# Expert blocks in order of their counts, narrow blocks with high and low halves side by side, their down projection in plain fp32

## The chip, the cores and the metric

One core of one Trainium2 chip runs the whole program. The metric is the device time of one execution in microseconds; three executions of the kernel before took 2009.57, 2016.96 and 2018.43 us (median 2016.96).

## The reference, cut to what matters

Two mixer layers (state space, window and forgetting attention), a third hybrid layer, and behind it a mixture of 32 experts over 256 tokens. The change is in the mixture alone, apart from the few steps just ahead of it:

```python
# t: 256 x 1024; w_gate, w_up: 32 x 1024 x 512; w_down: 32 x 512 x 1024
combine = two chosen experts of each token (softmax weights), zero for the other 30
for e in range(32):
    hid = silu(t @ w_gate[e]) * (t @ w_up[e])
    out = out + combine[:, e:e + 1] * (hid @ w_down[e])
```

So 512 (token, expert) pairs exist. Each expert's three matrices are 2 MB each and are read from HBM once for each block of rows that uses them.

## The kernel before

**Routing.** The 512 pairs are sorted by expert: VectorE counts the pairs of each expert (a matmul sums the one-hot rows), a scan gives each expert's offset, and `slots_of` makes two 256-column halves of a 0/1 matrix that says which token stands at which sorted place. TensorE (`select`, L1078) multiplies the tokens by it into `xs`: all 512 sorted rows, transposed, in a high and a low half of fp32r. The low half is what fp32r's rounding left over, so a product is three fp32r matmuls (hi by hi, hi by lo, lo by hi; L668 to L670).

**Blocks.** There are 35 blocks of 128 sorted rows: block x below 32 is the start of expert x, and three more (`route_more`) take the rows of experts with over 128. `move_window` copies the 128 columns of block x out of `xs` into one of two windows: the high half on ScalarE, the low half on VectorE.

**Units.** A block's step on TensorE has 12 units of weights, each [128 x 1024] floats (512 KB): 4 of `w_gate[x]` (i = 0 to 3), 4 of `w_up[x]` (i = 4 to 7), and 4 of `w_down` of the block before (i = 8 to 11). A unit is 6 matmuls of 512 columns: 2 k x 3 for gate and up (window stationary, weights moving), 2 output halves x 3 for down. At i = 2 the hidden rows of block x - 1 are transposed (`turn_hidden`, 4 transposes); at i = 3 ScalarE copies them as high half (`hid_hi`) and VectorE makes the low half (`hid_lo`); the down units at i = 8 wait for that.

**Halving.** ScalarE casts each unit's high half (`high_half`, L2415 with L2425), VectorE subtracts for the low half (`low_half`, L1835 with L1173). Both run through the steps in the program's order, 6 units (`LOOK`) ahead of TensorE; the ring of halves has 8 places. In a step ScalarE and VectorE do these in a fixed order: for VectorE the low half that is due, then (i = 8) the product of gate and up, then (i = 3) the hidden rows' low half.

**Loads.** SyncE issues every load, in order, 1 MB (two units) each, into 6 slots: for each x gate of x, up of x, down of x - 1 (`load_half`, L2750). A load waits until VectorE has halved both units that lay in its slot, which are the same matrix's of one block before. The first three loads are issued during the stage before (`bridge`, with the first 4 units halved there too), four more as buffers come free, before the routing is known.

**Output.** ScalarE and VectorE copy the two down banks; POOL scatters the rows to HBM (`store_rows`), and at the end gathers them; VectorE adds them with their weights.

Of the kernel before, what the change touches and what calls it, by code (L numbers as in the profile page):

```python
# [2 lines left out]

# [5 lines left out]
F32 = mybir.dt.float32  # L9
F32R = mybir.dt.float32r  # L10
BF16 = mybir.dt.bfloat16
I32 = mybir.dt.int32
# [40 lines left out]
MORE = 3  # L53
BLOCKS = EXP + MORE
SLOTS = 2 * S
SLOT_QUARTERS = SLOTS // 256
LAST_START = SLOTS - P
UNITS_OF = 12
N_UNITS = UNITS_OF * BLOCKS
RING, LOOK, EARLY = 8, 6, 4  # L60
# [143 lines left out]
def build(nc, d, out):  # L204
    ctx = ExitStack()
    with ctx:  # L206
# [57 lines left out]
        more_ready, hid_hi_made = (sem(n) for n in ("more_ready", "hid_hi_made"))  # L264
# [262 lines left out]
        def unit_halves(u):  # L527
            tiles = w_halves + [(y_hi, y_lo), (y_hi, y_lo), (h_hi, h_lo), (h_hi, h_lo)]
            hi, lo = tiles[u % RING]
            c = D if u % RING in (5, 7) else 0  # L530
            return hi[:, c:c + D], lo[:, c:c + D]

# [15 lines left out]
        def stationary(x):  # L548
            return tuple(a[:, :, 0:P] for a in xs) if x == 0 else windows[x % 2]
        hid = [R[1][:, i * FF:(i + 1) * FF] for i in range(2)]  # L550
# [5 lines left out]
        hid_t = [(over_tile(f"hid_hi{i}", FF, "r1", D + i * FF), over_tile(f"hid_lo{i}", FF, "r0", i * FF)) for i in range(2)]  # L556
        y_out = [merged[:, i * D:(i + 1) * D] for i in range(2)]
# [3 lines left out]
        more_hot = bias_rows[0][:, 0:96].rearrange("p (j e) -> p j e", j=MORE)  # L561
        of_expert = bias_rows[0][:, 96:204].rearrange("p (q e) -> p q e", q=3)
        offset, count = (of_expert[:, i, 0:EXP] for i in range(2))
        offset_all, count_all = (of_expert[:, i, 0:BLOCKS] for i in range(2))
# [3 lines left out]
        reach, over, rank = bias_rows[0][:, 432:464], bias_rows[0][:, 464:496], bias_rows[1][:, 80:112]  # L568
# [3 lines left out]
        more_wide = scratch[2][:, 0:3 * MORE * EXP].rearrange("p (q j e) -> p q j e", q=3, j=MORE)  # L572
        more_sums = bias_rows[1][:, 360:369].rearrange("p (q j) -> p q j", q=3)
        more_i = bias_rows[1][:, 372:372 + MORE].bitcast(I32)
# [4 lines left out]
        counting = consts[:, CH:2 * CH]  # L579
# [34 lines left out]
        def tensor_program(e):  # L614
# [448 lines left out]
            def moe():  # L1063
# [12 lines left out]
                e.matmul(bank[:, 2 * EXP:3 * EXP], ones, m1, start=False, stop=True).then_inc(full[b], 1)  # L1076
# [11 lines left out]
                def turn_hidden(x):  # L1088
                    await_drained(("up", x))
                    b, bank = take(turned, ("hid", x))  # L1090
                    for k in range(4):
                        done = e.transpose(bank[:, k * P:(k + 1) * P], hid[x % 2][:, k * P:(k + 1) * P], ident)
                    done.then_inc(full[b], 1)
# [3 lines left out]
                e.wait_ge(ht_lo_made, 2 * T)  # L1097
                early = Banks([0, 1, 2, 3, 4, 5, 6])
                for f in range(8):
                    select(0, f, early)  # L1100
                for x in range(BLOCKS + 1):
                    for i in range(units_in(x)):
# [14 lines left out]
                        e.wait_ge(m_lo, u + 1)  # L1117
                        hi, lo = unit_halves(u)
                        if x < BLOCKS and i < 8:
                            for j in range(2):  # L1120
                                k = 2 * (i % 4) + j
                                done = product(bank_up[:, :], tuple(a[:, k, :] for a in stationary(x)),
                                               (hi[:, j * FF:(j + 1) * FF], lo[:, j * FF:(j + 1) * FF]), k == 0, k == KD - 1)
                        else:
                            k = i % 4
                            for n, (b, bank) in enumerate(got):
                                done = product(bank[:, :], tuple(a[:, k * P:(k + 1) * P] for a in hid_t[(x - 1) % 2]),
                                               (hi[:, n * CH:(n + 1) * CH], lo[:, n * CH:(n + 1) * CH]), k == 0, k == 3)
# [29 lines left out]
        def vector_program(v):  # L1158
# [676 lines left out]
            def low_half(u):  # L1835
                v.wait_ge(m_hi, u + 1)
                hi, lo = unit_halves(u)
                tt(lo, unit_raw(u), hi.bitcast(F32), SUB, m_lo)
# [7 lines left out]
            def bridge():  # L1846
# [4 lines left out]
                for u in range(EARLY):  # L1851
                    low_half(u)
# [8 lines left out]
            def route():  # L1861
# [35 lines left out]
                o.did(v.tensor_copy(of_expert[:, 2, 0:EXP], index_row), mask_ready)  # L1897
                for q in range(len(QUARTERS)):
                    low_quarter(q)
                b, n, bank = await_full(("count",))  # L1900
                total = bank[:, T * EXP:(T + 1) * EXP]
                o.did(v.tensor_tensor_scan(reach, unit_row[:, 0:1].to_broadcast([P, EXP]), total, 0.0, MUL, ADD))
                o.did(v.tensor_copy(count, total))
                o.prev()
                tt(offset, reach, count, SUB)
                o.prev()
                tt(tok(place), tok(bank[:, 0:T * EXP]), offset.unsqueeze(1).to_broadcast([P, T, EXP]), ADD, drained[b], n)
                o.prev()
# [17 lines left out]
            def route_more():  # L1926

                ts(over, count, 128.0, None, ALU.is_gt)
                o.prev()
                o.did(v.tensor_tensor_scan(rank, unit_row[:, 0:1].to_broadcast([P, EXP]), over, 0.0, MUL, ADD))  # L1930
                o.prev()
                tt(rank, rank, over, MUL)
                o.prev()
                tt(more_hot, rank.unsqueeze(1).to_broadcast([P, MORE, EXP]), bc(unit_row[:, 0:MORE], EXP), ALU.is_equal)
                o.prev()
                tt(more_wide, of_expert[:, :, 0:EXP].unsqueeze(2).to_broadcast([P, 3, MORE, EXP]), more_hot.unsqueeze(1).to_broadcast([P, 3, MORE, EXP]), MUL)
                o.prev()
                o.did(v.tensor_reduce(more_sums, more_wide, AX, ADD))
                o.prev()
                ts(offset_all[:, EXP:BLOCKS], more_sums[:, 0, :], 128.0, None, ADD)  # L1940
                ts(count_all[:, EXP:BLOCKS], more_sums[:, 1, :], -128.0, None, ADD)
                o.did(v.tensor_copy(more_i, more_sums[:, 2, :]), more_ready)
                o.prev()

            def starts():

                ts(start_f, offset_all, float(LAST_START), None, MIN)
# [42 lines left out]
            def move_window(x):  # L1990
# [4 lines left out]
                start = v.value_load(start_i[0:1, x:x + 1], min_val=0, max_val=LAST_START)  # L1995
                if x >= 2:
                    v.wait_ge(m_used, first_unit(x - 2) + 8)
                v.tensor_copy(windows[x % 2][1], xs[1][:, :, bass.DynSlice(start, P)]).then_inc(window_lo, 1)

            def moe():  # L2000
# [3 lines left out]
                for f in range(1, 8, 2):  # L2004
                    fill(0, f)
                for u in range(EARLY, LOOK):
                    low_half(u)
                slots_of(1)
                route_more()
                starts()  # L2010
                weighing = weights()
                next(weighing)
                late = []
                for x in range(BLOCKS + 1):
                    for i in range(units_in(x)):
                        u = first_unit(x) + i
                        if u + LOOK < N_UNITS:
                            low_half(u + LOOK)
# [84 lines left out]
        def scalar_program(a):  # L2103
# [311 lines left out]
            def high_half(u):  # L2415
# [5 lines left out]
                elif u < 6:  # L2421
                    await_full((("out2", 1), 1))
                else:
                    await_full(("router",))
# [466 lines left out]
```

## Time and profile before

| | |
|---|---|
| median of 3 runs | 2016.96 us |
| profiled execution: its own time / its span | 2012.43 us / 2010.3 us |
| mixture: first product of block 0 / first of block 1 / end of the last | 1384.0 / 1403.7 / 1990.1 us from the span's start |
| TensorE busy, whole span | 94% |
| mean granted TensorE clock | 0.983 |
| read from HBM | 406.5 MB |

Slices 28 to 39 of the page's 40 (50 us each) are the mixture. "Busy" of TensorE is by modelled ends: a matmul's record overlaps the next, so the distance from start to start is its cost. The trace times count from the span's start.

### The profile page before, as it was taken

The numbers are of one execution on the slowest core, as the hardware profiler recorded it, in microseconds if no ns is written. First come the engines' busy times: TensorE is split into PE (matmuls) and PEld (weight loads), VectorE is DVE, ScalarE is ACT, GpSimd is POOL, SyncE is SP. The second block draws the span as 40 slices with busy tenths as digits, with TensorE's granted clock in tenths as the row PEclk, the third lists the DMA queues.
The fourth block names the chain that finished last, engine by engine and source line by source line (L and its number), as shares of the span: only waits on it lengthen the run. The fifth ranks groups of instructions, "written<-read, shape, count | busy, mean of one in ns | idle before, by whom it ended". The sixth has DMA issues, their size and how long they took to land. (4 is left out here: it accounts for less than half of the span.)

```text
span 2010.3 us, 24359 instructions
## 1 busy us (share of the span) xinstructions
PE 1898.1 (94%) x8814; PEld 1458.1 (73%) x8814; DVE 1429.7 (71%) x2063; ACT 1097.8 (55%) x1623; POOL 103.4 (5%) x98
## 2 busy tenths in 40 slices
PE   7998999999999899999999988896999999999995
PEld 6876777777887677777755445545888888888884
DVE  5968555455696856456647966337999999999994
ACT  5634555444563455544431122114888888888883
POOL 1000000000000000000011210000100000000001
PEclk9999999999999999999999999997999999999997
DMA  7633544345554443434553523155999999999993
GB/s 231 181 123 117 154 119 126 116 130 176 159 178 126 136 135 118 129 113 150 183 158 120 157 84 105 53 188 197 341 373 384 374 382 371 377 376 375 376 379 117
DMA packets 135751, 411.32 MB, mean 205 GB/s; under 512 B 17837, under 2 KB 19629, under 8 KB 108753
## 3 DMA queue, kind: packets, MB, share of 16 engines
q1 hardware_dynamic: 128768, 405.41, 59.0%
q0 software_dynamic: 6864, 4.36, 0.8%
q8 instruction: 71, 1.16, 0.2%
q14 instruction: 48, 0.39, 0.1%
HBM read 406.50 MB, written 19.47 MB: 212 GB/s over the span
## 5 line engine op out<-in xcount | busy, mean ns | idle before, releaser
L1173 DVE TENSOR_TENSOR w_lo<-w_raw,w_hi 128x1024 fp32r<-128x1024 f32 x372 | 444.9, 1216 | 224.8 <-ACT w_hi L2125 223.0
L2125 ACT CAST w_hi<-w_raw 128x1024 fp32r<-128x1024 f32 x266 | 277.4, 1047 | 158.6 <-PE bank L670 151.5
L668 PE MATMUL bank<-w_hi,h_hi 128*128 128x512 f32 x800 | 324.6, 406 | 14.4 <-DVE w_lo L1173 14.4
L670 PE MATMUL bank<-w_hi,h_lo 128*128 128x512 f32 x800 | 313.5, 392 | 0.0
L669 PE MATMUL bank<-w_lo,h_hi 128*128 128x512 f32 x800 | 312.7, 391 | 0.0
L668 PEld LDWEIGHTS bank<-w_hi,h_hi 128*128 128x128 f32 x800 | 150.9, 189 | 50.0 <-issue 14.4
L2296 ACT ACTIVATE r<-bank,small 128x256 f32<-128x256 f32 (+1 forms) x152 | 63.9, 425 | 204.9 <-DVE small L1176 204.9
L670 PEld LDWEIGHTS bank<-w_hi,h_lo 128*128 128x128 f32 x800 | 150.7, 188 | 33.2
L669 PEld LDWEIGHTS bank<-w_lo,h_hi 128*128 128x128 f32 x800 | 151.2, 189 | 28.6
L719 PE MATMUL bank<-w_raw,h_all 128*128 128x512 f32 (+1 forms) x320 | 142.3, 601 | 1.1 <-DVE h_all L1173 1.1
L1173 DVE TENSOR_TENSOR w_lo<-r,w_hi 128x1024 fp32r<-128x1024 f32 x106 | 124.7, 1218 | 25.1 <-ACT w_hi L2425 25.1
L719 PEld LDWEIGHTS bank<-w_raw,h_all 128*128 128x128 f32 x320 | 61.5, 194 | 72.1 <-issue 70.4
L2425 ACT CAST w_hi<-w_raw 128x1024 fp32r<-128x1024 f32 x106 | 110.0, 1057 | 6.6 <-PE bank L670 6.6
L2425 ACT CAST w_hi<-r 128x1024 fp32r<-128x1024 f32 x106 | 109.9, 1059 | 3.4 <-PE bank L670 3.4
L668 PE MATMUL bank<-w_hi,window_hi 128*128 128x512 f32 x272 | 107.9, 397 | 0.0
L670 PE MATMUL bank<-w_hi,window_lo 128*128 128x512 f32 x272 | 106.6, 392 | 0.0
L669 PE MATMUL bank<-w_lo,window_hi 128*128 128x512 f32 x272 | 106.4, 391 | 0.0
L668 PE MATMUL bank<-w_hi,y_hi 128*128 128x512 f32 x256 | 102.0, 398 | 0.0
L670 PE MATMUL bank<-w_hi,y_lo 128*128 128x512 f32 x256 | 99.9, 390 | 0.0
L669 PE MATMUL bank<-w_lo,y_hi 128*128 128x512 f32 x256 | 99.7, 390 | 0.0
L1463 DVE TENSOR_REDUCE small<-bank 128x2 f32<-128x512 f32 (+1 forms) x76 | 43.7, 576 | 58.6 <-PE bank L911 27.7
L1173 DVE TENSOR_TENSOR h_lo<-w_raw,h_hi 128x1024 fp32r<-128x1024 f32 x70 | 83.6, 1216 | 0.0
(357 smaller groups left out, 3680.9 us busy)
## 6 DMA issues: line engine op xcount, KB each, us to landing
w_raw<-in_w_in SPq DMA_DIRECT2D x236, 512.0 KB, 3.7
r<-in_w_up SPq DMA_DIRECT2D x69, 1024.0 KB, 7.4
w_raw<-in_w_gate SPq DMA_DIRECT2D x68, 1024.0 KB, 7.2
w_raw<-in_w_down SPq DMA_DIRECT2D x36, 1024.0 KB, 7.1
r<-in_w_down SPq DMA_DIRECT2D x34, 1024.0 KB, 7.3
w_raw<-in_w_proj SPq DMA_DIRECT2D x48, 512.0 KB, 3.7
w_raw<-in_w_out SPq DMA_DIRECT2D x24, 512.0 KB, 4.2
w_raw<-in_w_mem_kv SPq DMA_DIRECT2D x8, 512.0 KB, 4.1
```

The costliest lines, as they stand in the source:

```text
L668: e.matmul(out_, sh, mh, start=first, stop=False, skip_group_check=shared)
L669: e.matmul(out_, sh, ml, start=False, stop=False, skip_group_check=shared)
L670: return e.matmul(out_, sl, mh, start=False, stop=last, skip_group_check=shared)
L719: done = e.matmul(bank[:, 0:c.n], c.lhs[0][:, kk, t * P:(t + 1) * P], w[:, k, :], start=kk == 0, stop=kk == c.n_k - 1)
L1173: o.did(v.tensor_tensor(out_, a, b, op), sem, value)
L1463: o.did(v.tensor_reduce(mx, two[:, :, 0:keys_of(t)], AX, MAX))
L2125: a.copy(halves(n)[0], raw_of(n)).then_inc(w_hi, 1)
L2296: a.activation(p_buf[i % 2][:, j * keys:(j + 1) * keys], bank[:, 0:keys], ACT.Exp, bias=mx_all[:, c + j:c + j + 1], accum_out=sum_all[:, c ...
L2425: a.copy(unit_halves(u)[0], unit_raw(u)).then_inc(m_hi, 1)
```

## The change

The 35 blocks are ordered by their expert's count, the largest expert first. Ranks 0 to 2 get two blocks each, ranks 3 to 31 one. A rank r has at most 512 // (r + 1) rows, so `PAIRED` marks the blocks that cannot have more than 64 rows: block 5 (the second of rank 2) and blocks 10 to 34 (ranks 7 to 31), 26 of 35. Blocks 0 to 4 and 6 to 9 stay as they were.

In a paired block the window's high half of 64 rows and its low half of 64 rows lie side by side as one stationary tile of 128 columns. It is multiplied by the weights' high and then by their low half: 2 matmuls for each k, not 3. The two groups of 64 output rows are added later: `turn_hidden` multiplies gate rows and up rows (8 plain fp32 matmuls of 64 columns) by `stacked`, two identities on top of each other, in place of 4 transposes. ScalarE then applies silu to the turned gate, VectorE multiplies by the turned up. The down projection takes the result as [128 x 64] stationary and the loaded weights as they are, in fp32: 2 matmuls of 512 columns a unit, no halving (`whole_unit`).

The order is worked out by VectorE with one more matmul (`order`), and SyncE issues the first load only after it (`order_ready`); every load's address comes from a register. A slot that held down weights of a paired block is free when TensorE has used them (`m_used`), no longer when VectorE has halved them. Nothing is halved in the bridge any more: all first 6 units are halved in the mixture's own start.

```diff
+BLOCK_RANK = [0, 0, 1, 1, 2, 2] + list(range(3, EXP))
+BLOCK_SKIP = [0, P, 0, P, 0, P] + [0] * (EXP - 3)
+PAIRED = [min(S, 2 * S // (r + 1)) - skip <= P // 2 for r, skip in zip(BLOCK_RANK, BLOCK_SKIP)]
...
+        def whole_unit(u):
+            x, i = step_of(u)
+            return PAIRED[x - 1] and x > 0 and (i >= 8 or x == BLOCKS)
+        halved_units = [u for u in range(N_UNITS) if not whole_unit(u)]
+        def halves_due(u):
+            return range(*(min(halved_before[u + i] + LOOK, len(halved_units)) for i in range(2)))
```

On TensorE, `turn_hidden(x)` of a paired block, then the units:

```diff
+                        for j, rows_of in enumerate((gate_rows[x % 2], up_rows[x % 2])):
+                            for k in range(4):
+                                c = (4 * j + k) * P // 2
+                                done = e.matmul(bank[:, c:c + P // 2], rows_of[:, k * P:(k + 1) * P], stacked, start=True, stop=True)
...
+                        if whole_unit(u):
+                            k, raw = i % 4, unit_raw(u)
+                            e.wait_ge(in_moe[(u // 2) % 6], 16 * (u // 12 + 1))
+                            for n, (b, bank) in enumerate(got):
+                                done = e.matmul(bank[0:P // 2, :], hid_whole[(x - 1) % 2][:, k * P // 2:(k + 1) * P // 2],
+                                                raw[:, n * CH:(n + 1) * CH], start=k == 0, stop=k == 3)
...
+                                    if PAIRED[x]:
+                                        both_halves = windows[x % 2][0][:, k, :]
+                                        e.matmul(bank_up[:, :], both_halves, hi[:, cols], start=k == 0, stop=False)
+                                        done = e.matmul(bank_up[:, :], both_halves, lo[:, cols], start=False, stop=k == KD - 1)
```

On ScalarE, then on VectorE, step i of block x:

```diff
                         if x and i == (3 if x < BLOCKS else 0):
+                            if PAIRED[x - 1]:
+                                a.activation(gate_t[(x - 1) % 2], bank[:, 0:FF // 2], ACT.Silu).then_inc(hid_hi_made, 1)
...
-                        if u + LOOK < N_UNITS:
-                            high_half(u + LOOK)
+                        for n in halves_due(u):
+                            high_half(n)
...
+                        for n in halves_due(u):
+                            low_half(n)
...
                         if x and i == (3 if x < BLOCKS else 0):
+                            if PAIRED[x - 1]:
+                                tt(hid_whole[(x - 1) % 2], gate_t[(x - 1) % 2], bank[:, FF // 2:FF], MUL, drained[b], n)
```

On VectorE, the start of the mixture:

```diff
+                low_quarter(3)
+                fill(0, 1)
+                fill(0, 3)
+                low_half(0)
+                fill(0, 5)
+                fill(0, 7)
+                low_half(1)
                 slots_of(1)
-                route_more()
+                tt(stacked, ident[:, 0:P // 2], ident[:, P // 2:P], ADD, stacked_made)
+                low_half(2)
                 starts()
+                for n in range(3, LOOK):
+                    low_half(n)
```

On SyncE, the wait in `load_half`, the loads dropped from the bridge, and the loop:

```diff
                 if n >= 6:
-                    s.wait_ge(m_lo, 2 * (n - 5))
+                    u = 2 * (n - 6)
+                    s.wait_ge(*((m_used, u + 2) if whole_unit(u) else (m_lo, halved_before[u + 2])))
...
-                for kind, j in (("w_gate", 0), ("w_gate", 1), ("w_up", 0)):
-                    load_half(0, kind, j)
...
+            s.wait_ge(order_ready, 1)
+            before_it = None
+            for x in range(BLOCKS + 1):
+                expert = s.value_load(expert_i[0:1, x:x + 1], min_val=0, max_val=EXP - 1) if x < BLOCKS else None
+                for y, kind in ((expert, "w_gate"), (expert, "w_up"), (before_it, "w_down")):
+                    for j in range(2 if y is not None else 0):
+                        load_half(y, kind, j)
+                before_it = expert
```

## Rows read from the trace of the kernel before

**Rows 1.** The page's 40 slices of the span.
```profile
PE   7998999999999899999999988896999999999995
DVE  5968555455696856456647966337999999999994
PEclk9999999999999999999999999997999999999997
```
**Rows 2.** Busy time by stretch; columns PE, PEld, DVE, ACT, POOL, PEclk, DMA share, GB/s.
```profile
1600.00:1700.00 100.00, 100.00 (x451) 82.22 (x450) 91.57 (x89) 86.73 (x101) 6.80 (x6) 1.00 1.00 377
```
**Rows 3.** SyncE's queue in order of time: start us, us.
```profile
1462.91 0.33 SPq L2758 DMA_DIRECT2D r<-in_w_down  x1
...
1603.34 3.80 SPq L2758 DMA_DIRECT2D w_raw<-in_w_gate  x2
...
1953.22 0.33 SPq L2758 DMA_DIRECT2D r<-in_w_down  x1
```
**Rows 4.** TensorE around the start of one block, in order of time.
```profile
1602.63 0.39 PE L668 MATMUL bank<-y_hi,hid_hi 128*128 128x512 f32 x1
...
1608.08 0.39 PE L668 MATMUL bank<-w_hi,window_hi 128*128 128x512 f32 x1
...
1610.86 0.60 PE L1092 MATMUL bank<-consts,r 128*128 128x128 f32 x4
```
**Rows 5.** Plain fp32 matmuls: one line by source, then two runs by time.
```profile
L719 PE MATMUL bank<-w_raw,h_all x320: 542/592/1167, 1042.6 to 1250.1; 128*128 128x512 f32 x144, 128*128 128x452 f32 x16
...
1331.99 14.00 PE L719 MATMUL bank<-w_raw,y_all 128*128 128x512 f32 x32 [1.14 <-DMA w_raw<-in_w_out]
...
1354.01 1.87 PE L1046 MATMUL bank<-r,h_all 128*128 128x36 f32 x16
```
**Rows 6.** Four loads in a burst: issues, median us to landing; last, the page's.
```profile
1359.47 0.82 SPq L2758 DMA_DIRECT2D w_raw<-in_w_gate  x2
1360.34 1.12 SPq L2758 DMA_DIRECT2D r<-in_w_up  x2
...
w_raw<-in_w_gate SPq DMA_DIRECT2D x1, 1024.0 KB, 5.1
...
r<-in_w_up SPq DMA_DIRECT2D x1, 1024.0 KB, 11.7
...
w_raw<-in_w_gate SPq DMA_DIRECT2D x68, 1024.0 KB, 7.2
```
**Rows 7.** ScalarE and VectorE at work on halves and hidden rows, in order of time.
```profile
1609.24 2.01 ACT L2425 CAST h_hi<-r 128x1024 fp32r<-128x1024 f32 x2
1610.33 2.36 DVE L1173 TENSOR_TENSOR h_lo<-r,h_hi 128x1024 fp32r<-128x1024 f32 x2 [1.28 <-ACT h_hi L2425]
...
1612.09 0.60 ACT L2478 CAST hid_hi<-bank 128x512 fp32r<-128x512 f32 x1
```
**Rows 8.** TensorE's waits and granted clock (stretches: PE busy, PEclk).
```profile
1982.76 0.50 PE L668 MATMUL bank<-w_hi,hid_hi 128*128 128x512 f32 x1 [2.01 <-DVE hid_lo L1173]
...
1980.00:1983.00 3.00, 0.99 (x7) 1.00 0.00 0
1983.00:1986.50 3.50, 3.50 (x10) 0.54 0.02 0
...
1329.00:1333.00 4.00, 2.86 (x8) 1.00 1.02 384
```
**Rows 9.** The start of the mixture, in order of time.
```profile
1336.71 4.62 DVE L1173 TENSOR_TENSOR w_lo<-r,w_hi 128x1024 fp32r<-128x1024 f32 x4
...
1363.33 0.16 DVE L1173 TENSOR_TENSOR small<-small 128x2 f32<-128x2 f32 x1
...
1375.49 0.88 DVE L1179 SCALAR_TENSOR_TENSOR slots<-consts,bias,slots 128x256 fp32r<-128x256 f32 x2
...
1383.97 0.50 PE L668 MATMUL bank<-w_hi,xs_hi 128*128 128x512 f32 x1 [0.78 <-DVE xs_lo L1988]
...
1403.71 0.40 PE L668 MATMUL bank<-w_hi,window_hi 128*128 128x512 f32 x1
```

More of the change, by code:

```diff
@@ L2 @@
 from dataclasses import dataclass
+import itertools
 import numpy as np
@@ L567, in build @@
         place = bias_rows[0][:, 368:432]
-        reach, over, rank = bias_rows[0][:, 432:464], bias_rows[0][:, 464:496], bias_rows[1][:, 80:112]
+        key = bias_rows[0][:, 432:464]
         placed = bias_rows[1][:, 112:240].rearrange("p (c e) -> p c e", c=2)
@@ L1075, in moe @@
                 e.matmul(bank[:, 2 * EXP:3 * EXP], ones, m0, start=True, stop=False)
-                e.matmul(bank[:, 2 * EXP:3 * EXP], ones, m1, start=False, stop=True).then_inc(full[b], 1)
+                e.matmul(bank[:, 2 * EXP:3 * EXP], ones, m1, start=False, stop=True)
+                e.matmul(bank[0:EXP, 3 * EXP:3 * EXP + 1], m0, ones[:, 0:1], start=True, stop=False)
+                e.matmul(bank[0:EXP, 3 * EXP:3 * EXP + 1], m1, ones[:, 0:1], start=False, stop=True).then_inc(full[b], 1)
+                e.wait_ge(order_in, 4)
+                b, bank = take(turned, ("order",))
+                e.matmul(bank[:, 0:EXP + 3 * BLOCKS], ones[0:EXP, :], order_cols, start=True, stop=True).then_inc(full[b], 1)
                 def select(q, f, ring=chosen_banks):
@@ L1096, in moe @@
                 e.wait_ge(ht_hi_made, 2 * T)
-                e.wait_ge(ht_lo_made, 2 * T)
-                early = Banks([0, 1, 2, 3, 4, 5, 6])
-                for f in range(8):
+                early = Banks([5, 6, 2, 3, 4, 0, 1])
+                for n, f in enumerate(FIRST_FILLS):
+                    if n == 2:
+                        e.wait_ge(ht_lo_made, 2 * T)
                     select(0, f, early)
@@ L1903, in route @@
+                stt(key, total, 64.0, key, MUL, ADD)
+                stt(key_col, total_col, 64.0, lane[0:EXP, :], MUL, ADD)
+                o.did(v.tensor_copy(count_col, total_col))
                 o.did(v.tensor_copy(count, total))
                 o.prev()
-                tt(offset, reach, count, SUB)
+                ts(ahead, key[0:EXP, :], key_col, None, ALU.is_gt)
+                o.prev()
+                o.did(v.tensor_reduce(rank_col, ahead, AX, ADD))
+                tt(ahead_count, ahead, count[0:EXP, :], MUL)
@@ L1924, in slots_of @@
                         slots_ready if t == T - 1 else None)
[L1926 to L1943, printed above, removed]
             def starts():
-                ts(start_f, offset_all, float(LAST_START), None, MIN)
+                tt(start_f, offset_all, block_last, MIN)
                 o.prev()
@@ L2444, in bridge @@
                 yield
-                for u in range(EARLY):
-                    high_half(u)
                 yield
@@ L2460, in moe @@
                     high_quarter(q)
-                for u in range(EARLY, LOOK):
-                    high_half(u)
                 for f in range(0, 8, 2):
                     fill(0, f)
+                for n in range(LOOK):
+                    high_half(n)
                 late = []
```

184 lines of the change are left out of this document (102 added, 82 removed).

## The prediction

> **What bounds the kernel now.** I read the 40 slices first, then busy time by stretch, then SyncE's queue and TensorE's timeline over one block, and last the waits and the granted clock. The slices show TensorE and VectorE at nine tenths from slice 29 on, clock at its top, with one flat stage up to slice 38 [rows 1]; this is the mixture, and outside of it the change touches only the steps just ahead. In 100 us of it TensorE is busy all the time and DMA moves 377 GB/s at a share of 1.00 [rows 2]. Both look full, so a block is read from both sides. SyncE's load of the first down half comes again after (1953.22 - 1462.91) / 29 = 16.91 us [rows 3]. TensorE's 24 down matmuls take 1608.08 - 1602.63 = 5.45 us, 0.227 each, so a block of 72 is 16.3, and the four transposes take about 0.5 [rows 4]: 16.9, the whole period. So TensorE sets the pace. The loads would allow a little less: in a burst the first lands 5.1 us after its issue at 1359.47 and the fourth 11.7 after its issue at 1361.13, which is (1372.83 - 1364.57) / 3 = 2.75 us for each further MB [rows 6], 16.5 us for a block's six.
>
> **What TensorE does in a paired block.** Gate and up: 32 matmuls for 48, 32 x 0.227 = 7.3 us, -3.6. Down: 8 fp32 matmuls of 512 columns. Line 719 is plain fp32; it shows 320 records where the program has 10 chunks x 16 = 160 matmuls, and 32 records take 14.0 us, 0.43 each [rows 5]. A plain matmul is thus two records, 0.86 us, and the down projection 8 x 0.86 = 6.9 us for 5.45, +1.4. Had a 64-column stationary tile only half the price, it would be 3.4; the nearest rows have 128 columns, and what streams is the 512 columns either way, so I take 6.9. Turning the hidden rows: 8 matmuls of 64 columns; 16 records (8 matmuls) of 36 columns took 1.87 us [rows 5], so 1.9 for 0.5, +1.4 (bounds: 1.0 by the transposes' rate, 2.5). Sum 16.1 us, 0.8 less than now. VectorE loses 4 low halves of 1.18 and ScalarE 4 casts of 1.0 [rows 7]; neither was the bound, worth nothing by itself.
>
> **What the new waits do.** This decides. The slot of down(x-2)'s second half is now free only when TensorE has used it, at the end of block x-1; call that time 0. Before, VectorE had halved it six units ahead. SyncE is in order, so gate(x+1), though its slot has long been free, is queued behind that load. Now it is asked for 1608.08 - 1603.34 = 4.7 us ahead of the block's start [rows 3, 4]; after the change it is asked for about 1 us behind it. It is wanted early: at step i = 2 ScalarE must cast gate(x+1)'s first unit, and behind that, in program order, stands the silu of the hidden rows; VectorE has the low halves of the first and the second unit ahead of the hidden product; and TensorE's down(x-1) waits for that product. The chain, with 0.1 for each hop from engine to engine:
>
> - the load of down(x-1)'s second half issued at 0.25, landed at 0.25 + 5.1 = 5.35; gate(x+1) first half next in the queue, + 2.75 = 8.1 [rows 6]
> - ScalarE: cast 1.0, silu of 256 columns 0.4 (0.60 for 512 [rows 7], most of the price fixed), cast 1.0: 10.6
> - VectorE: low half of the second unit 1.2, product 0.4: 12.3
> - TensorE: down 6.9 and a hop: 19.3, which is the next time 0.
>
> TensorE's own work up to the down is 7.3 + 1.9 = 9.2 us, so it stands idle some 3.1 us in each block. Bounds of the chain: with the hops at nothing (0.4) and the second load half a microsecond faster than the burst's average 18.4; if the gate load takes the 7.2 that the steady state shows [rows 6] behind an issue at 1.1, with a hop for reading the expert's number into a register (a read that no row prices; 0 to 1.5 us), 19.9.
>
> Then the clock. At the end of the run TensorE waited once for exactly this, the hidden rows: 2.01 us idle after dense work, and in the next 3.5 us the granted clock was 0.54, the lower level of 1.2 GHz, and matmuls cost double; 1.1 us of idle at 1331 left it at 1.00 [rows 8]. A wait of 3.1 us in every block will mostly do the same. It costs half of about 3.4 us, 1.7, and lies in the down matmuls, on the chain: 21.0 us. I take it in four blocks of five, so 20.7 on average.
>
> The chain holds where down(x-2), down(x-1) and the gate and up of x are all paired and there is a gate(x+1): x = 12 to 33, 22 blocks. 22 x (20.7 - 16.9) = +84 us.
>
> The Trainium skill ("SBUF — State Buffer", section "The DMA setup-cost knee") gives a transfer as a fixed 2 us and its bytes at 436 GB/s. For a pair of 1 MB loads an estimate from it is 2 + 2 x 2.4 = 6.8 us where the rows give 5.1 + 2.75 = 7.85; by the page the chain would be 1.05 shorter and the time 23 us lower. This kernel's own landings decide here.
>
> The other blocks. Blocks 5 and 10 have paired gate and up before an unpaired down (-3.6 each); blocks 6 and 11 follow with turn and down at the new price (+2.8; block 11 has the paired gate too, -3.6). TensorE alone would gain 5 of it, but the loads' 16.5 a block and the same held-up hidden rows in blocks 7 and 11 take most back: 0 in sum (bounds -5 and +5). Block 34 has no gate behind it, -0.8; the last down has the dearer turn and matmuls, +2.8, and shorter copies, -0.5: +1.5 together. The first transfer after TensorE (scatter, gather, sum) stays.
>
> **The start of the mixture.** It loses its early work. Four low halves that stood in a gap of VectorE during the stage before (4.6 us [rows 9]) now come after the routing; with them go the casts and seven early loads. The order adds some 20 small VectorE operations at about 0.2 with their waits (0.16 busy [rows 9]), 13 of them and a round trip over TensorE ahead of `slots`; `route_more`, ten such operations, goes. I put the slots matrix 2.4 us later than 1376.4, and order_ready at about 1375.5, so the first load lands near 1381, ahead of the end of the 8 selecting groups, which moves from 1384.0 to 1386.4: the loads hide, the halving does not. VectorE's extra work from there on is 4.6 for the low halves less 2 for `route_more` and about 1 of fill-waits. Block 1 would start at 1403.7 + 6 [rows 9]. Bounds: 2 (only the slots' delay; VectorE's new work falls into its waits for the selecting matmuls) and 11 (everything in series). Without the selecting as cover the loads' landing would cost up to another 4.
>
> **The sum**, against the profiled execution (2012.4 us, span 2010.3; the median of the runs shown is 4.5 above it): +6 start, 0 blocks 1 to 11, +84 blocks 12 to 33, +1.5 end: 2012.4 + 91 = 2104. I say 2102.
>
> **The rivals.**
>
> *The chain without the clock.* The idle of 3 us does not bring the clock down, or in few blocks; the chain is 19.3. 22 x 2.4 = 53, + 7.5: 2073. For it: the single row at 1.1 us, and that the clock looks different with 9 us of work between two waits. Against: 2.01 us were enough. The Trainium skill ("TensorE: Matmul & The Clock Gate", section "HAM oscillation — how this bites in real kernels") has a loop whose wait for loads throttles TensorE again in every round; by that rule it is 22 blocks of 22, 22 x 0.3 = 7 us above my sum.
>
> *No chain: TensorE or the loads set the pace.* The gate load lands before ScalarE's cast is due, or the hidden rows pass it. The block is then 16.1 by TensorE, 16.5 by the loads. 24 blocks x (16.3 - 16.9) = -14, + 7.5, and -2 for the small rest: 2004 (1999 with 16.1 throughout). Faster. It decides from a landing of gate(x+1) at about 5 us after time 0 instead of 8.1. For it: nothing in the rows beside the lone landing of 5.1. Against: the order of SyncE, ScalarE and VectorE in the program.
>
> *fp32 down at half the price* (one record of 0.43 for each 64-column matmul). The chain is 12.3 + 3.4 + 0.1 = 15.8 plus the wait; below 16.5, so the loads set the pace or, where the clock still falls, the chain at some 17: 2008 to 2020, most likely 2012. No change.
>
> *Loads that get slower in bursts.* SyncE now asks for four or five MB at once. In the steady state single landings reach 7.2 [rows 6] though they are evenly asked for; if the burst's landings stretch by that much, the chain is 22 or more, 22 x 5.3 + 7.5: 2136.
>
> **How the numbers follow.** Chain with the clock 0.58 (its own range 2085 to 2115), chain without 0.20, no chain 0.10, half price 0.05, slower loads 0.07. For 8 times in 10 the range goes from 2052 (chain 18.4 without the clock: 22 x 1.5 + 7) to 2130. A measurement of this kernel tells about 0.5% (10 us) from no change: faster 0.09, same 0.06, slower 0.85.
>
> **What would show it.** In the trace after: SyncE issues one down load near the end of a block, then down, gate, gate, up at once; TensorE's longest waits are at the down matmuls, for VectorE's product, about 3 us in each of 22 blocks; ScalarE waits about as long for `w_gate` loads; PEclk falls to 8 or 9 tenths from slice 31 on; the block's period is 20 to 21 us, and DMA falls to some 300 GB/s. Wrong if TensorE stays without waits and the period is 16 to 17 (no chain), if the down units of a paired block show 8 records and not 16 (half price), or if the period is near 19.3 with PEclk at 9 (no clock).

## The result, and the profile after

The changed kernel takes 2113.15 us (median of 4 runs, 2110.76 to 2120.18) where the kernel before takes 2014.82 (4 runs): 1.0492 times as long, 95% interval 1.0466 to 1.0519, or 98 us more.

The profiled execution took 2120.18 us, 7 above the median. That is not the mixture's doing: the same small copy on VectorE, the last step ahead of the counting, starts 8.40 us later than before, in code that did not change. In the 12 versions of the experiments below the same copy starts between 1367.38 and 1377.51, though none of their edits reaches ahead of it; 8.3 of the 8.4 us are there before 1250 us already (one and the same matmul at 1240.96 before, at 1249.24 after), ahead of the loads that the change drops.

```profile
1368.87 0.18 DVE L1897 COPY bias<-consts 128x32 f32<-128x32 f32 x1
```
```profile
1377.27 0.18 DVE L1949 COPY bias<-consts 128x32 f32<-128x32 f32 x1
```

So the 107.8 us more in the span are 8.4 ahead of the mixture and 99.4 in it, and times of the mixture are compared after taking 8.4 off.

The page's slices after, the answer to [rows 1]: in the last ten slices but one (from 1589 us on) TensorE reads 8 for 9 and VectorE 5 or 4 for 9. The clock reads 8 in three of these nine (a 9 is 90% or more); the rows below have it in numbers.

```profile
PE   8989999999998999999999898879998888888885
DVE  5967555556776655566579663389895454545452
PEclk9999999999999999999999899989999999898898
GB/s 229 169 130 129 129 117 139 98 160 152 187 159 90 161 118 127 116 149 163 169 125 151 79 111 60 87 306 363 342 407 306 321 297 305 281 299 299 277 323 142
```

The same 100 us as in [rows 2], and the next 100: in the first, TensorE is idle for 13.5 us, the clock is 0.92 for 1.00, and DMA moves 317 GB/s for 377.

```profile
1600.00:1700.00 100.00, 86.55 (x312) 49.65 (x311) 52.01 (x55) 50.58 (x65) 4.51 (x5) 0.92 0.82 317
1700.00:1800.00 100.00, 88.19 (x317) 50.39 (x315) 47.19 (x50) 44.57 (x58) 5.46 (x5) 0.91 0.78 297
```

One block of 64 rows, all engines, weight loads and the even run of gate and up matmuls left out. Time 0 is 1705.59, TensorE's first matmul of the block.

```profile
1705.59 0.50 PE L1174 MATMUL bank<-y_hi,window_hi 128*128 128x512 f32 x1
1705.69 0.33 SPq L2822 DMA_DIRECT2D w_raw<-in_w_down  x1
...
1706.78 1.29 SPq L2822 DMA_DIRECT2D w_raw<-in_w_gate  x2
...
1707.56 1.00 PE L1131 MATMUL bank<-consts,r 128*128 128x64 f32 x8
...
1708.17 2.30 SPq L2822 DMA_DIRECT2D r<-in_w_up  x2
1708.40 1.06 PE L1131 MATMUL bank<-consts,up_rows 128*128 128x64 f32 x8
1709.27 0.48 PE L1174 MATMUL bank<-h_hi,window_hi 128*128 128x512 f32 x1
...
1713.98 1.05 ACT L2486 CAST y_hi<-w_raw 128x1024 fp32r<-128x1024 f32 x1 [5.33 <-DMA w_raw<-in_w_gate]
...
1714.94 0.38 ACT L2539 ACTIVATE gate_t<-bank 128x256 f32<-128x256 f32 x1
1715.07 2.44 DVE L1227 TENSOR_TENSOR y_lo<-w_raw,y_hi 128x1024 fp32r<-128x1024 f32 x2 [4.96 <-ACT y_hi L2486]
1715.21 1.03 ACT L2486 CAST y_hi<-w_raw 128x1024 fp32r<-128x1024 f32 x1
...
1717.42 0.41 DVE L1227 TENSOR_TENSOR hid_whole<-gate_t,bank 128x256 f32<-128x256 f32 x1
...
1717.89 5.12 PE L1164 MATMUL bank<-r,hid_whole 128*64 128x512 f32 x8 [2.78 <-DVE hid_whole L1227]
```

The reader is to see the order on each queue. The second down half is asked for 0.10 us after time 0 and both gate halves behind it, where [rows 3] and [rows 4] had the gate 4.7 us ahead of the block. The turned rows are in the bank at about 1709.5 (1708.40 + 1.06), but ScalarE sits in the cast of the next gate's first unit, waits 5.33 us for its landing, and only then does the silu; VectorE does two low halves and then the product; TensorE waits 2.78 us and runs its first 8 down records in 5.12 us.

The waits of the whole mixture, by engine: total us, times, longest.

```profile
ACT y_hi L2486 <- DMA w_raw<-in_w_gate: 123.7, 24, 6.5
...
PE bank L1164 <- DVE hid_whole L1227: 66.5, 23, 4.0
```

The last of these 23 is the end of the run, 1.00 us. The other 22 are of 2.24 to 4.00 us, 2.98 on average, and each is followed by slow down matmuls: the first 8 records took 5.1 to 6.6 us, where the other 8 of the same block took 3.60. Three of the 22:

```profile
1614.20 5.34 PE L1164 MATMUL bank<-r,hid_whole 128*64 128x512 f32 x8 [3.34 <-DVE hid_whole L1227]
1619.38 3.60 PE L1164 MATMUL bank<-w_raw,hid_whole 128*64 128x512 f32 x8
...
1634.66 5.34 PE L1164 MATMUL bank<-r,hid_whole 128*64 128x512 f32 x8 [2.24 <-DVE hid_whole L1227]
...
1889.37 6.42 PE L1164 MATMUL bank<-r,hid_whole 128*64 128x512 f32 x8 [4.00 <-DVE hid_whole L1227]
```

The granted clock around the block above: 2.80 us of idle, then 3.5 us at 0.57, close to the lower level of 1.2 GHz, then full again. It is the fall of [rows 8] repeated in the middle of the mixture (columns as in [rows 2]).

```profile
1715.10:1717.90 2.80, 0.02 (x2) 0.01 (x1) 2.80 (x4) 2.57 (x4) 0.00 (x0) 0.93 1.01 427
1717.90:1721.40 3.50, 3.50 (x5) 1.10 (x6) 3.50 (x4) 3.48 (x5) 0.00 (x0) 0.57 0.64 272
1721.40:1726.50 5.10, 5.10 (x13) 1.49 (x12) 1.94 (x3) 0.10 (x2) 0.00 (x0) 1.00 0.49 154
```

**The ledger.** GpSimd scatters each block's rows once, so its 35 issues date the blocks. Block x's rows are scattered after the down matmuls, and these stand at the end of the step of block x + 1. So from the scatter of block 10 to that of block 32 run the steps of blocks 12 to 33, the 22 for which the prediction has the chain. Before, then after: the scatters of blocks 0, 10, 32 and 34.

```profile
1424.42 5.88 POOL L2608 DMA_INDIRECT y_rows<-merged,bias  x1 [61.72 <-ACT merged L2475]
...
1593.40 0.97 POOL L2608 DMA_INDIRECT y_rows<-merged,bias  x1 [16.06 <-ACT merged L2475]
...
1965.49 0.96 POOL L2608 DMA_INDIRECT y_rows<-merged,bias  x1 [14.86 <-ACT merged L2475]
...
1991.65 0.97 POOL L2608 DMA_INDIRECT y_rows<-merged,bias  x1 [8.43 <-DVE merged L2045]
```
```profile
1436.93 5.90 POOL L2675 DMA_INDIRECT y_rows<-merged,bias  x1 [65.83 <-ACT merged L2535]
...
1603.53 0.91 POOL L2675 DMA_INDIRECT y_rows<-merged,bias  x1 [12.17 <-ACT merged L2535]
...
2073.16 0.90 POOL L2675 DMA_INDIRECT y_rows<-merged,bias  x1 [20.07 <-ACT merged L2535]
...
2099.09 0.90 POOL L2675 DMA_INDIRECT y_rows<-merged,bias  x1 [8.73 <-DVE merged L2109]
```

- To block 0's scatter: 12.51 - 8.40 = +4.1 us.
- From there to block 10's, the steps of blocks 2 to 11: 166.60 for 168.98, -2.4.
- The 22 to block 32's: 469.63 for 372.09, +97.5, or 21.35 us a block for 16.91.
- The rest, block 34 and the end: +0.1.

The sum is 99.4 but for rounding.

### The profile page after: what moved, and what is told of

It reads as the page before. It is cut to its first block and busy times, and to the rows that moved or that the text cites. A ratio compares the mean times of both kernels' runs of the same rounds, so it can differ in the third digit from the quotient of the medians.

```text
span 2118.1 us, 23790 instructions
## 1 busy us (share of the span) xinstructions
PE 1936.7 (91%) x8508; PEld 1367.6 (65%) x8508; DVE 1303.1 (62%) x1964; ACT 980.8 (46%) x1519; POOL 104.8 (5%) x98
## 5 line engine op out<-in xcount | busy, mean ns | idle before, releaser
L1227 DVE TENSOR_TENSOR w_lo<-w_raw,w_hi 128x1024 fp32r<-128x1024 f32 x296 | 356.3, 1217 | 229.4 <-ACT w_hi L2189 227.5
L2189 ACT CAST w_hi<-w_raw 128x1024 fp32r<-128x1024 f32 x266 | 277.4, 1047 | 167.9 <-PE bank L697 159.5
L695 PE MATMUL bank<-w_hi,h_hi 128*128 128x512 f32 x800 | 327.1, 409 | 15.2 <-DVE w_lo L1227 13.9
L1227 DVE TENSOR_TENSOR w_lo<-r,w_hi 128x1024 fp32r<-128x1024 f32 x130 | 153.3, 1221 | 137.9 <-ACT w_hi L2486 137.6
L1164 PE MATMUL bank<-r,hid_whole 128*64 128x512 f32 x200 | 133.5, 831 | 65.5 <-DVE hid_whole L1227 65.5
L1227 DVE TENSOR_TENSOR y_lo<-w_raw,y_hi 128x1024 fp32r<-128x1024 f32 x58 | 70.4, 1224 | 113.4 <-ACT y_hi L2486 113.4
L1164 PEld LDWEIGHTS bank<-r,hid_whole 128*64 128x64 f32 x200 | 34.9, 186 | 151.3 <-issue 76.0
L2486 ACT CAST w_hi<-r 128x1024 fp32r<-128x1024 f32 x130 | 130.5, 1049 | 1.5 <-PE bank L697 0.8
L2486 ACT CAST y_hi<-w_raw 128x1024 fp32r<-128x1024 f32 x58 | 60.2, 1045 | 123.8 <-DMA w_raw<-in_w_gate 123.7
L2535 ACT COPY merged<-bank 64x512 f32<-64x512 f32 (+1 forms) x68 | 36.2, 583 | 147.9 <-PE bank L1164 137.6
L1164 PE MATMUL bank<-w_raw,hid_whole 128*64 128x512 f32 x216 | 97.0, 592 | 1.0 <-DVE hid_whole L1227 1.0
```

The lines of the kernel that those rows point to most:

```text
L695: e.matmul(out_, sh, mh, start=first, stop=False, skip_group_check=shared)
L1164: done = e.matmul(bank[0:P // 2, :], hid_whole[(x - 1) % 2][:, k * P // 2:(k + 1) * P // 2], raw[:, n * CH:(n + 1) * CH], start=k == 0, st ...
L1227: o.did(v.tensor_tensor(out_, a, b, op), sem, value)
L2189: a.copy(halves(n)[0], raw_of(n)).then_inc(w_hi, 1)
L2486: a.copy(unit_halves(n)[0], unit_raw(u)).then_inc(m_hi, 1)
L2535: a.copy(y_out[x % 2][0:rows_of, n * CH:(n + 1) * CH], banks[b][0:rows_of, :]).then_inc(drained[b], 1)
```

## The experiments

Each ratio is to the kernel before, measured beside it on the same chip: 2014.82 us for the changed kernel, then 2015.70 for the next four rows, 2015.59 for the four after them, 2016.84 for the last four.

| kernel | us, median | ratio to before, 95% | us a block, 12 to 33 |
|---|---|---|---|
| after | 2113.15 | 1.0492 (1.0466 to 1.0519) | 21.35 |
| hidden rows first | 2030.92 | 1.0083 (1.0060 to 1.0106) | 17.36 |
| gate loads ahead, all blocks | 2037.99 | 1.0109 (1.0078 to 1.0141) | 16.47 |
| halves 5 ahead | 2058.77 | 1.0216 (1.0175 to 1.0257) | 18.65 |
| halves 4 ahead | 2005.29 | 0.9955 (0.9938 to 0.9972) | 16.54 |
| order only | 2021.53 | 1.0029 (1.0016 to 1.0042) | 16.92 |
| clock kept | 2082.78 | 1.0332 (1.0309 to 1.0355) | 19.43 |
| gate ahead and halves 4 ahead | 2008.74 | 0.9960 (0.9944 to 0.9976) | 16.37 |
| halves 4 ahead, less down | 2006.13 | 0.9958 (0.9943 to 0.9973) | 16.72 |
| gate ahead, paired blocks | 2008.12 | 0.9957 (0.9941 to 0.9973) | 16.55 |
| before, halves 4 ahead | 2009.16 | 0.9967 (0.9950 to 0.9984) | 16.92 |
| order only, halves 4 ahead | 2016.42 | 0.9997 (0.9983 to 1.0012) | 16.92 |
| gate ahead, 4 ahead, less down | 1977.60 | 0.9813 (0.9780 to 0.9846) | 15.25 |

The last column is (scatter of block 32 less scatter of block 10) / 22 in the profiled execution. The versions with "less down" leave out a part of the output.

### Is it the chain? Three ways to open it

**The hidden rows first.** On both engines the step for the hidden rows moves ahead of the halves; of the edit only ScalarE's line is shown, and VectorE's does the same.

```diff
-                        if x and i == (3 if x < BLOCKS else 0):
+                        if x and i == (0 if x == BLOCKS else 2 if PAIRED[x - 1] else 3):
```

> In the blocks of 64 rows the hidden rows are finished first: ScalarE's silu and VectorE's product of gate and up stand at step 2, ahead of the halves of the next gate's first unit, instead of at step 3 behind them; loads, their order, the plain fp32 products and the turns stay. Theory A (the chain through the load order and the two in-order engines, and the clock that falls in its wait): a block goes from 21.35 us to TensorE's own work, 32 x 0.227 + 1.7 + 16 x 0.45 = 16.2 to 16.9; over 22 blocks 98 to 113 us less, 2000 to 2015 us, TensorE's waits for VectorE's product gone and the clock at 0.97 or more after 1600 us. Rival B (the plain fp32 products and the 16 turns themselves are too dear): the product is early and nothing is won, 2105 to 2120. Rival C (the six loads of a block can't be had in less than 20 us once all are by number and late): 2100 to 2120, with SyncE's loads landing later than before they are wanted. Rival D (the wait is real, but the clock stays low in such blocks for another reason): the 66 us of waits go, the clock stays at 0.9: 2040 to 2055.

Measured: 82 us less than the changed kernel (2030.92), and in the profiles the 22 blocks have 88 us less. The waits for the hidden rows are gone (1.0 us, the last block's), and the clock is at 1.00 from 1500 to 1900 us, so rival D falls. It is theory A's result, but 16 to 31 us short of its size, and the waits say why:

```profile
PE bank L1174 <- DVE window_hi L2050: 23.8, 16, 2.4
```

The gate load is as late as ever. Behind its casts in ScalarE's and VectorE's order stand also the copies of the next block's window, and now TensorE waits for those at the start of the block. One late load had two ways to reach TensorE; with the first closed the second shows. Of these waits 22.9 us lie in the 23 blocks from 12 to 34, which take 401.64 us; without them that would be 16.47 us each, close to the 16.37 of a block that waits for nothing (gate ahead and halves 4 ahead).

**The load order.** SyncE issues gate(x+1) ahead of down(x-1).

```diff
-                for y, kind in ((expert, "w_gate"), (expert, "w_up"), (before_it, "w_down")):
+            for kind, x in [("w_gate", 0), ("w_up", 0), ("w_gate", 1)] + [load for x in range(1, BLOCKS + 1) for load in (("w_up", x), ("w_gate", x + 1), ("w_down", x - 1))]:
```

> SyncE issues the two gate loads of block x+1 ahead of the two down loads of block x-1; slots, the order of ScalarE and VectorE and all arithmetic stay. Theory A: the gate's landing no longer begins at the end of the block before (the slot that the first down half waits for), so its cast and all behind it is early; the product is made at about 4 to 6 us of the block and not at 12.3: a block of 16.2 to 17 us, total 2000 to 2020 us, the same as with the hidden rows first. Rival B (fp32 work): 2105 to 2120. Rival C (bandwidth): 2100 to 2120, since the same 6 MB go in every block. A further rival, E (the down halves, now the last to be landed, become the wait: their issue at time 0, two landings of 5.2 and 7.9 us): still covered, since the down products begin at about 9 us; if the second is late a stall of under 1 us in each of 22 blocks, 2020 to 2040.

Measured: from block 13 on the blocks of 64 rows go to 16.36 us (block 12 takes 18.6), TensorE busy all the time (100.00 of 100 from 1700 to 2000 us, DMA 374 to 389 GB/s), as theory A has it. The time is above its range, because the expectation counted the late blocks alone: the ten before went from 16.7 us in the changed kernel to 19.7 (block 10's scatter at 1632.21 less block 0's at 1435.54, by 10). In these ten the down halves are still cast, and put last they came late:

```profile
ACT w_hi L2486 <- DMA r<-in_w_down: 19.1, 4, 6.3
ACT y_hi L2486 <- DMA r<-in_w_down: 17.1, 4, 5.5
...
PE bank L695 <- DVE hid_lo L1227: 12.0, 6, 5.9
```

So it was tried again with the new order in the blocks with whole down halves alone:

```diff
+                ahead_of_down = [("w_gate", x + 1)] if PAIRED[x - 1] else []
+                issue += [load for load in [("w_gate", x), ("w_up", x)] + ahead_of_down + [("w_down", x - 1)] if load not in issue]
```

> As the changed kernel (halves six ahead), with the next gate's loads ahead of the down loads only in the blocks whose down halves are used whole; the eleven blocks before keep their order of loads, which cost 17 to 20 us of waits when it was changed for them too (2038 us). Theory A: the 2038 less these 20 to 25 us, 2010 to 2018 us, a block of 16.3 to 16.5 us and no wait for the hidden rows. If the lead of six units holds something by itself: over 2025.

Measured: 2008.12 us, 105 less than the changed kernel, by nothing but the order of gate and down loads on one queue, and a little better than expected. Block 12 costs 20.2 us, the other 21 of the 22 blocks 15.9 to 16.8.

**The lead of the halves.** `LOOK`, how many units ahead halves are made, sets the step in which the next gate's first unit falls due.

```diff
-RING, LOOK = 8, 6
+RING, LOOK = 8, 5
```

> The halves are made five units ahead instead of six, in all blocks. Theory A: the next gate's first unit falls into step 3, behind the silu on ScalarE but still ahead of the product on VectorE. The chain is then load 8.1, cast 1.0, low half 1.2, product 0.4, down 7.0: 1.6 us shorter, still the longest: 22 x 1.6 = 35 us less, 2070 to 2085 us, a wait of some 1.2 us left at the down products. Theories B and C: no change, 2105 to 2120. Against all of them: halves made later could free slots later, which would show as a longer time than now.

```diff
-RING, LOOK = 8, 6
+RING, LOOK = 8, 4
```

> The halves are made four units ahead, in all blocks. Theory A: the next gate's first unit falls into step 4, behind silu and product on both engines, so the chain is open: 2000 to 2020 us, unless the shorter lead lets TensorE wait for halves (up to 0.5 us in each of 34 blocks, 17 us more). Theories B and C: 2105 to 2120.

Five ahead gave 54 us less than the changed kernel where I expected 28 to 43; four ahead gave 2005.29, at the low end of its range. The three lengths 21.35, 18.65 and 16.54 follow the place of one cast, with its low half, in the order. With five ahead a block lost 2.70 us and not 1.6: 1.24 of it is wait (38.3 us in the 22 blocks for 65.5), and 1.46 is the clock, which came back in part. The waits were 0.95 to 3.40 us long, and after most the down records ran at full speed:

```profile
1664.86 3.65 PE L1164 MATMUL bank<-r,hid_whole 128*64 128x512 f32 x8 [1.10 <-DVE hid_whole L1227]
...
1721.18 3.65 PE L1164 MATMUL bank<-r,hid_whole 128*64 128x512 f32 x8 [3.40 <-DVE hid_whole L1227]
...
1739.57 5.34 PE L1164 MATMUL bank<-r,hid_whole 128*64 128x512 f32 x8 [1.86 <-DVE hid_whole L1227]
```

Of its 22 waits 6 were followed by slow records (10.1 us more in all), of the changed kernel's 22 all (42.3 us more).

Rivals B (the fp32 work itself) and C (bandwidth) fall with these runs: arithmetic and bytes are the same in all of them.

### What the clock costs by itself

Three plain fp32 matmuls more in each of the 25 blocks with whole down weights (6 and 11 to 34), into a bank that nobody reads, ahead of the wait.

```diff
+                            if PAIRED[x - 1] and x < BLOCKS:
+                                for _ in range(3):
+                                    e.matmul(banks[7][:, :], ones, consts[:, 0:CH], start=True, stop=True)
                             await_drained(("hid", x - 1))
```

> The changed kernel with three more plain fp32 matmuls of 512 columns (ones by a constant, into a bank that nothing reads) in each of the 22 blocks, ahead of TensorE's wait for the hidden rows: 3 x 0.86 = 2.6 us of work in a wait of some 3 us. If the clock is a term of its own (theory A): the granted clock after 1600 us goes from 0.90 to 0.97 or more, the down products take 16 x 0.45 = 7.2 us instead of up to 8.8, and the block goes from 21.35 to 19.3 to 20.0 us: 22 x 1.4 to 2.0 = 30 to 45 us less, 2068 to 2083 us, although TensorE has more to do. Rival D' (the clock costs nothing that the wait does not hide): 2110 to 2120. Rival H (the added work delays the down products more than the clock gives back): 2120 or more.

Measured: 2082.78 us, 30 less with more to do. TensorE's own wait is now 0.65 us in this block, and the down records after it run at full speed, as they do in all the others:

```profile
1728.76 2.74 PE L1160 MATMUL bank<-consts 128*128 128x512 f32 x6
...
1731.68 0.41 DVE L1230 TENSOR_TENSOR hid_whole<-gate_t,bank 128x256 f32<-128x256 f32 x1
...
1732.15 3.65 PE L1167 MATMUL bank<-r,hid_whole 128*64 128x512 f32 x8 [0.65 <-DVE hid_whole L1230]
```

The product of the hidden rows is as late as before (theory A's chain still stands, 19.43 us a block against a predicted 19.3), so 21.35 - 19.43 = 1.9 us a block was the clock, the same as the 42.3 / 22 = 1.92 that the slow records show. That is 42 us in the 22 blocks; some 8 of them are paid back by the added matmuls in blocks 6, 11 and 34, where TensorE had nothing to wait for. This is a price, not a cure: the order of work gives 105.

### What the order of the experts costs, and what pairing gives

No block paired; the experts still in order, all weights by number and late (not shown: the last block's copies take all rows again).

```diff
-PAIRED = [min(S, 2 * S // (r + 1)) - skip <= P // 2 for r, skip in zip(BLOCK_RANK, BLOCK_SKIP)]
+PAIRED = [False] * BLOCKS
```

> Only the first half of the change: experts in order of their counts, loads from the registers, every block of 128 rows with split products as before (no block is paired). Theory A: blocks as before at 16.91 us, the later start alone, 3.4 us at the first product of block 1 in the trace of the changed kernel against the one before: 2017 to 2021 us. Rival F (the dynamic loads, with a register read of 0.76 us ahead of each gate pair, slow every block): 35 x up to 0.76 us = 27 us, 2040 us. Rival G (the order costs nothing beside the blocks): 2013 to 2016.

Measured: 2021.53, 1.0029 times before: 5.9 us, and the blocks at 16.92, so all of it is the start (rival F, the register reads, falls, and so does G). In the profile the start alone is 5.0 us longer. The interval leaves 3 to 8 us.

> Experts in order of their counts, every block of 128 rows with split products, halves four units ahead: against the version with blocks of 64 rows and the same lead (2005) it gives what those 22 blocks are worth in themselves. By the blocks' lengths, 16.9 us against 16.3 to 16.4: 22 x 0.5 to 0.6 = 11 to 14 us, so 2016 to 2021 us, the same as with six ahead (2021.5).

Measured: 2016.42. Against the 2005.29 with pairs and the same lead, pairing is worth 11 us. The two were not measured side by side, but their profiles agree: 10.1 us from the copy ahead of the counting to the end, of them 22 x (16.92 - 16.54) = 8.4 in blocks 12 to 33 and 2.4 ahead of them.

> The kernel before with halves four units ahead instead of six and nothing else. TensorE was busy in the whole of its blocks; theory A: no change, 2011 to 2020 us, and the gain of the fixed version is then the paired blocks' own. Rival: the shorter lead is itself the gain, about 10 us less, 2005.

A miss: I expected no change, and the interval excludes that: 2009.16, 0.9967 times before (0.9950 to 0.9984), 7.7 us less. Its blocks are not shorter. In the profiles 4.9 us of the gain are at the start, where two casts and two low halves fewer stand ahead of the copies of selected rows; TensorE's longest wait for them went from 4.55 us to 1.47, before and then with four ahead:

```profile
1399.83 1.22 PE L1084 MATMUL bank<-slots,ht_lo 128*128 128x256 f32 x4 [4.55 <-DVE xs_lo L1988]
```
```profile
1396.54 0.74 PE L1084 MATMUL bank<-slots,ht_lo 128*128 128x256 f32 x4 [1.47 <-DVE xs_lo L1988]
```

and 1.6 at the end, where the last two scatters are 7.8 us apart for 9.4. The best version, 2005.29, is thus made of the shorter lead (-7.7 us), the order (2016.42 - 2009.16 = +7.3) and the pairs (-11). Most of the 10 us by which it beats the kernel before needs no pairs: 2005.29 and 2009.16 were not measured side by side, the intervals of their ratios overlap, and no run here tells them apart.

### What holds the repaired block

> Halves four units ahead, and in the blocks whose down halves are used whole SyncE issues the next gate ahead of them; the blocks before keep their order of loads. If a block of 64 rows is now held by what TensorE has to do or by the loads' rate (16.2 us at 389 GB/s), nothing is left to win but the single stalls of 0.6 to 1.2 us for window and halves: 2000 to 2005 us. If the order of loads still held something in each block (0.3 us in 22): 1995 to 2000. If the down halves, now landed last, become a wait: 2010 or more.

Measured: 2008.74, both repairs together are no better than either. The blocks are at 16.37 for 16.54 us, but block 11, where the order of loads changes, costs 20.3 for 16.4, which takes it back. Is it TensorE or the loads that hold 16.37? Two kernels with less for TensorE to do, which leave out a part of the output:

```diff
-                                done = e.matmul(bank[0:P // 2, :], hid_whole[(x - 1) % 2][:, k * P // 2:(k + 1) * P // 2],
-                                                raw[:, n * CH:(n + 1) * CH], start=k == 0, stop=k == 3)
+                                cols = CH if k < 3 else 8
+                                done = e.matmul(bank[0:P // 2, 0:cols], hid_whole[(x - 1) % 2][:, k * P // 2:(k + 1) * P // 2],
+                                                raw[:, n * CH:n * CH + cols], start=k == 0, stop=k == 3)
```

> Halves four units ahead, and the last quarter of each down product of the blocks of 64 rows cut to 8 columns (that part of the output is left out): 2 plain fp32 matmuls or 4 records of 0.43 us = 1.7 us less of TensorE's work in each of 22 blocks. If TensorE's work holds the block of 16.3 us: 14.6 us, 22 x 1.7 = 37 us less, 1965 to 1975 us. If the six loads hold it (6.29 MB at 385 to 389 GB/s = 16.2 to 16.3 us): 2000 to 2007, and TensorE waits 1.5 us in each block for halves or for down loads. Between them if loads can go at up to 400 GB/s: 1990.

Measured: 2006.13, no gain, which looked like the loads' limit. Its waits said otherwise: 28.6 us of TensorE's time for the window, in 16 blocks, as in the kernel with the hidden rows first. With a shorter down projection the late gate load was too late again. This kernel did not tell what it was made for, so the same cut was made with the gate loads ahead:

> The version with halves four ahead and the gate loads first in the blocks of 64 rows (2008.7, blocks of 16.4 us with TensorE busy for all of them and loads at 390 to 395 GB/s), with the last quarter of each down product cut to 8 columns (that part of the output is left out): 1.7 us less work for TensorE in a block. If TensorE alone holds these blocks: 14.7 us, 37 us less, 1970 to 1975 us. If the loads can't go faster than about 390 to 400 GB/s: 15.7 to 16.2 us, 1990 to 2005 us, and TensorE waits 1 to 1.5 us in each block for data.

Measured: 1977.60, 31 us less than the same kernel with its whole down projection, 15.25 us a block, DMA at 414 to 420 GB/s from 1600 to 1900 us:

```profile
1600.00:1700.00 100.00, 98.41 (x425) 63.31 (x425) 67.47 (x73) 63.82 (x85) 7.26 (x7) 1.00 1.01 420
```

So TensorE holds the repaired block, with 16.37 us of work, and the loads' limit is no nearer than about 15.2, where TensorE first waits for down loads (8.1 us in 19 of the 22 blocks; 1.1 us gained a block and 0.4 waited are 1.5 of the 1.7 taken away). The rival of the expectation, a floor of the loads at 390 to 400 GB/s, falls.

## Why the prediction was right, and where its sizes were off

**The new wait: right, and as drawn.** In the block shown the cast of the next gate began 8.4 us after time 0 (1713.98 - 1705.59) for a predicted 8.1, the product ended at 12.2 (1717.42 + 0.41 - 1705.59) for 12.3, and TensorE stood 2.98 us on average for 3.1. The experiments show it as the cause from three sides, since each of these edits left arithmetic and bytes alone.

**TensorE's own work: right, a little small.** Per block 21.35 - 2.98 (wait) - 1.92 (slow records: 42.3 us over 3.65 each in 22 blocks) = 16.45 for a predicted 16.1. Gate and up took 1.97 + 5.84 = 7.8 us up to the wait in the block shown, for 7.3. Down matmuls are 16 records of 0.45 and not 8, so the rival of half price fell; the turns took 1.7 us (1709.27 - 1707.56) for 1.9.

**The clock: right mechanism, too small a term.** I took 1.7 us in four blocks of five, 1.4 on average (the row of [rows 8] itself, 3.5 us at 0.54, gives 1.6); it was 1.92 in all 22 by the records, and 1.9 by the version with the clock kept. 22 x (1.92 - 1.36) = 12 us, the largest error. The Trainium skill ("TensorE: Matmul & The Clock Gate", section "HAM oscillation — how this bites in real kernels") has the wait in every round throttle in every round; by that rule the forecast would have been 7 us higher, and here the trace agrees, 22 of 22. The kernel with five ahead shows that waits of 0.95 to 3.40 us did not all do so.

**The landings.** For two queued 1 MB loads the rows gave 7.85 us; measured, from the issue of the down half at 1705.69 to the cast at 1713.98, it was 8.3 with a hop. The Trainium skill ("SBUF — State Buffer", section "The DMA setup-cost knee") gives 6.8 by an estimate from its fit, which would have made the time 23 us lower; the trace does not agree with it.

**How many blocks.** I counted 22, x = 12 to 33, and there are 22: the waits stand in exactly these, and block 34 is back at 16.30 us. The ten steps before took 2.4 us less for a predicted 0: block 6 paid back what block 5 had gained (34.4 us together for 33.8), but block 10 came down from 16.8 to 13.8 us and block 11 took 16.8 for 17.0, so the hidden rows did not hold them up as the prediction had it.

**Start and end.** The start took 4.1 us more in the profile, and 5.0 in the profile of the version with the order only, for a predicted 6; block 34 and the end +0.1 for 1.5.

In sum: 4.1 - 2.4 + 97.5 + 0.1 = 99.4 (but for rounding) for a predicted 91.5. The 22 blocks are 13.5 above their 84, 12 of it the clock; start, early blocks and end are 6 below theirs, so part of the clock's error was made up by luck. The time lies in the range, and in the likeliest case's own.

**What the prediction left out.** The second way by which the same late load reaches TensorE, through the window copies, was not in it. It cost nothing while the first held, but decided what a repair gives: 2031 instead of 2008.

## What to carry to other kernels

When a change lets a buffer be freed later, look at what stands behind the load of that buffer in its queue, and then at what stands behind the first use of that second load on each in-order engine: here the gate loads, asked for 6 us later in the block, cost some 100 us, and another order of the loads, or halves made two steps later, gave them back. Close the cause (the late load), not the wait that shows: with the hidden rows moved ahead, the same load held TensorE by another instruction. And before a version is called a gain, try its tuning step on the kernel before too: 7.7 of the 10 us belonged to it.

## What was unexpected of the hardware

Loads from HBM went at 376 to 379 GB/s in the mixture before, where the DMA share read 0.99 to 1.00, at 390 to 395 with a share of 1.00 in the version with both repairs, and at 414 to 420 with a share of 1.01 when TensorE had less to do; a share of 1.00 in such a row was not the limit.

Waits of like length do not all bring the clock down: in the kernel with five ahead one of 1.86 us was followed by 8 records in 5.34 us and one of 3.40 by 8 in 3.65, both at the same place of a block. What tells them apart stays open.
